# The lead-in of a hybrid GLA/Hyena layer rearranged: no identity products, a fourth ada buffer, filters and spectra later, eight shift pieces moved to the gate stage

## What is computed

```python
sh1, sc1, g1, sh2, sc2, g2 = modulation(c, w_ada, b_ada)     # silu(c) @ w_ada + b_ada, w_ada is 2048 x 12288
csh1, csc1, ... = modulation(c_ctx, w_ada, b_ada)
hc = rmsnorm(ctx, norm_pre_mix) * (1 + csc1) + csh1           # context: k, v and decay only
hx = rmsnorm(x, norm_pre_mix) * (1 + sc1) + sh1
x = x + g1 * rmsnorm(mixer(hx, states(hc)), norm_post_mix)    # mixer: h @ w_in (2048 x 10272), then
#   GLA branch, Hyena branch (filters from a sine network, long convolution through a DFT),
#   merge gates, p_gla, p_hy, w_out
hx = rmsnorm(x, norm_pre_ffn) * (1 + sc2) + sh2
x = x + g2 * rmsnorm((silu(hx @ ffn_gate) * (hx @ ffn_up)) @ ffn_down, norm_post_ffn)
```

## Time and profile before

| | us |
|---|---|
| median of three runs | 1625.83 (1625.36 to 1626.21) |
| the profiled execution | 1625.28 |
| its span, first to last instruction | 1623.5 |
| PE busy | 1587.5 (98%) |
| DVE busy | 1101.5 (68%) |
| ACT busy | 749.4 (46%) |
| mean granted clock of PE | 0.995 |

### The profile page before, as it was taken

How to read it: one execution, slowest core, us unless ns; L and a number is a source line. 1 busy time by engine, 2 the same in 40 slices (tenths; PEclk the granted TensorE clock), 3 DMA queues, 4 the chain that set the end, 5 groups by cost and what they waited for, 6 DMA issues and landing times.

```text
span 1623.5 us, 22521 instructions
## 1 busy us (share of the span) xinstructions
PE 1587.5 (98%) x8524; PEld 1302.6 (80%) x8524; DVE 1101.5 (68%) x1320; ACT 749.4 (46%) x901; POOL 81.0 (5%) x156
## 2 busy tenths in 40 slices
PE   6999999999999999999998999999999999999998
PEld 3556677888888888888887888888888888888886
DVE  3677777678789868778777666666666555555556
ACT  5442326643444434444446544555545544444444
POOL 0011120000000000100000000000000000000000
PEclk9999999999999999999999999999999999999999
DMA  9989958666577768966885777777776665565653
GB/s 332 327 299 379 326 191 280 187 202 202 178 244 222 229 200 267 297 225 217 292 298 178 233 237 231 244 230 235 237 234 198 186 191 197 193 193 192 194 193 121
DMA packets 264769, 377.74 MB, mean 233 GB/s; under 512 B 14161, under 2 KB 223420, under 8 KB 263164
## 3 DMA queue, kind: packets, MB, share of 16 engines
q1 hardware_dynamic: 243008, 297.57, 58.2%
q0 software_dynamic: 20800, 78.91, 14.3%
q10 hardware_dynamic: 892, 0.33, 0.1%
HBM read 372.57 MB, written 4.19 MB: 232 GB/s over the span
## 4 chain that ended last, share of the span: by engine, by line
PE 92%; DVE 3%; DMA 2%; ACT 1%; issue 1%; ACTq 0%; DVEq 0%
PE ps L1664 39%; PE ps L1671 19%; PE ps L1679 9%; PE ps L1681 8%; PE ps L1680 8%; PE ps L1604 2%; DMA a2k<-in_w_ada 1%; DVE acck L1048 1%; PE ps L1803 1%; PE ps L1815 0%; PE ps L1594 0%; PE ps L1841 0%; DVE lo L1116 0%; PE ps L1766 0%; PE ps L1833 0%
## 5 line engine op out<-in xcount | busy, mean ns | idle before, releaser
L1441 DVE TENSOR_TENSOR lo<-raw,hi 128x1024 fp32r<-128x1024 f32 x252 | 308.3, 1224 | 247.9 <-ACT hi L879 247.5
L1664 PE MATMUL ps<-hx,hi 128*128 128x512 f32 x1392 | 438.0, 396 | 1.5 <-DVE lo L1441 0.8
L879 ACT ACTIVATE hi<-raw 128x1024 fp32r<-128x1024 f32 x252 | 266.7, 1060 | 317.0 <-PE ps L1671 203.9
L625 ACT ACTIVATE hi<-raw 128x1024 fp32r<-128x1024 f32 x224 | 236.6, 1060 | 277.9 <-PE ps L1671 163.9
L1664 PE MATMUL ps<-hxc,hi 128*128 128x512 f32 x1088 | 346.0, 399 | 0.0
L1116 DVE TENSOR_TENSOR lo<-raw,hi 128x1024 fp32r<-128x1024 f32 x224 | 269.5, 1220 | 67.3 <-ACT hi L625 67.2
L1671 PEld LDWEIGHTS ps<-hx,lo 128*128 128x128 f32 x1408 | 264.5, 188 | 62.5
L1671 PE MATMUL ps<-hx,lo 128*128 128x256 f32 x1408 | 276.6, 278 | 0.0
L1671 PEld LDWEIGHTS ps<-hxc,lo 128*128 128x128 f32 x1088 | 204.4, 188 | 48.3
L1664 PEld LDWEIGHTS ps<-hx,hi 128*128 128x128 f32 x1392 | 212.0, 189 | 2.8 <-DVE lo L1441 1.0
L1671 PE MATMUL ps<-hxc,lo 128*128 128x256 f32 x1088 | 213.9, 278 | 0.0
(11 more groups left out here) (323 smaller groups left out, 1685.8 us busy)
## 6 DMA issues: line engine op xcount, KB each, us to landing
raw<-in_w_in SPq DMA_DIRECT2D x160, 512.0 KB, 4.6
a2raw<-in_w_ada POOLq DMA_DIRECT2D x96, 512.0 KB, 5.1
raw<-in_ffn_gate SPq DMA_DIRECT2D x88, 512.0 KB, 4.4
raw<-in_ffn_up SPq DMA_DIRECT2D x88, 512.0 KB, 4.4
raw<-in_ffn_down SPq DMA_DIRECT2D x88, 512.0 KB, 4.6
ada_raw<-in_w_ada SPq DMA_DIRECT2D x64, 512.0 KB, 10.1
a2k<-in_w_ada POOLq DMA_DIRECT2D x32, 512.0 KB, 6.7
raw<-in_w_out SPq DMA_DIRECT2D x32, 512.0 KB, 5.3
```

Of the source, the lines that this page charges most:

```text
L625: nc.scalar.activation(high_of(uu), raw[:, slot_of(uu), :], ACT.Copy).then_inc(hi_done, 1)
L879: nc.scalar.activation(hi[:, slot, :], raw[:, uu % RING, :], ACT.Copy).then_inc(hi_done, 1)
L1441: V.tensor_tensor(lo[:, uu % RING, :], raw[:, uu % RING, :], hi[:, uu % 4, :].bitcast(f32), SUB).then_inc(lo_done, 1)
L1664: mm(bank(b + t), (hi[:, uu % 4, :] if w_h is None else w_h)[:, c0:c0 + P], feat[:, k, :], start=first, stop=False)
```

## The change

It rearranges the lead-in and the kv stage:

- The 24 identity products (`keep_running`) go. Ada unit 0 comes ahead of the second turn, the turns of the first tokens come behind ada unit 2, and the third sine step moves behind the second kv piece.
- `ada_raw` gets a fourth buffer, used by ada unit 3 alone, in a part of the weight ring not yet in use; SP issues four ada units at once, and its order through block 1 is written out.
- Filter pairs 0 and 1 stand behind kv pieces 4 and 6 of block 1, pairs 2 and 3 in block 2; the eight spectra start at piece 5 of block 2. Filter tiles shrink to half. The stores of the spectra have a semaphore each.
- In block 0 to 2, ada units, turns and columns are placed anew; on DVE `columns(b+1)` comes ahead of the low part and the a2 piece at the same place.
- Only 24 of the 32 shift pieces stay in the kv stage, from block 2 on. The last eight become pieces 56 to 63 with a sum of their own (`acck2`), in the gate stage: `A2_AT` has 20 pieces on units 137 to 157, where it had 13 on units 138 to 158, 3 on 162 to 182 for 5, and 17 on 192 to 217 for 14 on 198 to 218. Eight more column sums and one DVE operation at the FFN's start bring them in.

```diff
-        A2_KV = [(), (7, 9, 11), (1, 3, 5, 7, 9, 11), (1, 3, 5, 7, 9, 11), (1, 9, 11),
-                 (1, 3, 5, 7, 9, 11), (1, 3, 5, 7, 9, 11), (1, 3)]
+        A2_KV = [(), (), (7, 9, 11), (1, 4, 6, 9, 11), (1, 4, 9, 11), (0, 1, 2, 4, 9, 11),
+                 (2, 6, 10), (1, 2, 4)]
         A2_AT = ([28 + int(2.4 * a) for a in range(19)] + [81, 86, 91, 96, 99, 102, 105, 108, 110, 112, 119, 121, 123]
-                 + [138 + int(1.7 * a) for a in range(13)] + [160 + 6 * a for a in range(5)]
-                 + [198 + int(1.6 * a) for a in range(14)])
+                 + [137 + int(1.1 * a) for a in range(20)] + [162, 172, 182]
+                 + [192 + int(1.6 * a) for a in range(17)])
...
-        AFTER = [{3: "a", 5: "xa", 7: "at", 8: "a", 9: "c"},
-                 {2: "a", 4: "a", 6: "a", 8: "a", 9: "tc"},
-                 {0: "a", 1: "at", 3: "a", 5: "a", 7: "c", 10: "a"}]
+        AFTER = [{5: "axa", 7: "at", 8: "a", 9: "c"},
+                 {1: "a", 3: "a", 5: "a", 7: "a", 8: "t", 9: "c"},
+                 {0: "a", 1: "a", 3: "a", 5: "a", 6: "t", 7: "c", 10: "a"}]
...
-        FILT_AFTER = [{}, {0: 0, 2: 1, 4: 2, 6: 3}] + [{}] * (NB - 2)
-        SPEC_AFTER = {0: 0, 1: 1, 2: 2, 3: 3, 4: 4, 6: 5, 8: 6, 11: 7}
+        FILT_AFTER = [{}, {4: 0, 6: 1}, {1: 2, 3: 3}] + [{}] * (NB - 3)
+        SPEC_AFTER = {(2, 5): 0, (2, 6): 1, (2, 7): 2, (2, 8): 3, (2, 9): 4, (2, 10): 5, (2, 11): 6,
+                      (3, 0): 7}
...
+        def ada_slot(n):
+            return n if n < 4 else (n - 4) % 3
...
             pool.wait_ge(t_sem["a"], upto(START, "a", startno("sine", 2)))
-            pool.wait_ge(kv_pe, 12)
+            pool.wait_ge(kv_pe, 20)
             pool.dma_start(cp[:, K_FWD:K_SEL], k_pack[:, K_FWD:K_SEL]).then_inc(s_fwd, 16)
+            pool.wait_ge(kv_pe, 26)
-            for a in range(7):
+            for a in range(4):
                 a2_load(a)
...
-                if b == 5:
+                if b == 6:
                     ins = shift_sums(16)
...
+                for j in range(8):
+                    ins = mm(bank(0)[:, KD + j:KD + j + 1], acck2[:, P * j:P * (j + 1)],
+                             ones[:, 0:1], start=True, stop=True)
...
             start_step("turn", 0)
+            pe.wait_ge(t_sem["a"], 1)
+            ada_unit(0)
             start_step("turn", 1)
             start_step("sine", 0)
-            pe.wait_ge(t_sem["a"], 1)
-            ada_unit(0)
-            keep_running(4)
             ada_unit(1)
-            keep_running(4)
             start_step("sine", 1)
+            ada_unit(2)
             turn_tokens(0, range(2))
             turn_tokens(1, range(2))
-            ada_unit(2)
-            keep_running(6)
             ada_unit(3)
-            keep_running(2)
-            start_step("sine", 2)
             columns(0)
-            keep_running(8)
```

More of the change, by code:

```diff
@@ L199, in layer @@
         s_win = sem("s_win")
-        ada_in = [sem(f"ada_in{i}") for i in range(3)]
+        ada_in = [sem(f"ada_in{i}") for i in range(4)]
         ada_mm, ada_rows = sem("ada_mm"), sem("ada_rows")
@@ L215, in layer @@
         a2_done = sem("a2_done")
-        s_wgz, s_kks, s_kkl, s_inv = sem("s_wgz"), sem("s_kks"), [sem(f"s_kkl{i}") for i in range(2)], sem("s_inv")
+        s_wgz, s_kks, s_kkl, s_inv = sem("s_wgz"), [sem(f"s_kks{i}") for i in range(2)], [sem(f"s_kkl{i}") for i in range(2)], sem("s_inv")
         s_row = [sem(f"s_row{i}") for i in range(4)]
@@ L426, in weight_load, with filter_load @@
                 sp.dma_start(dst, srcw).then_inc(arrival(uu)[0], 16)
-            for n in range(3):
+            def filter_load():
+                for half in range(2):
+                    sp.dma_start(outw[HID * half:HID * (half + 1), :],
+                                 out_w[:, HY * half:HY * (half + 1)]).then_inc(s_win, 16)
+                sp.dma_start(win[:], k_win.rearrange("(t p) n -> p t n", p=P)).then_inc(s_win, 16)
+            for n in range(4):
                 ada_load(n)
-            ada_load(3)
             weight_load(0)
@@ L435, in _ @@
             sp.dma_start(toks[:, 3, :], ctxt[P:2 * P, :]).then_inc(s_ctx[1], 16)
-            for b in range(NB - 1):
+            for n in range(4, 8):
+                ada_load(n)
+            weight_load(3)
+            ada_load(8)
+            ada_load(9)
+            weight_load(4)
+            filter_load()
+            ada_load(10)
+            weight_load(5)
+            ada_load(11)
+            weight_load(6)
+            weight_load(7)
+            sp.dma_start(lrw[:], w_in.rearrange("(k p) n -> p k n", p=P)
+                         [:, :, C_LR:C_LR + 2 * RANK]).then_inc(s_lrw, 16)
+            weight_load(8)
+            for b in range(2, NB - 1):
                 for n in range(3):
@@ L517, in _ @@
             pool.wait_ge(kv_ev, 12 * (NB - 1))
-            for a in range(32, 53):
+            for a in range(NKS, 45):
                 a2_load(a)
@@ L532, in _ @@
             pool.dma_start(grow[:], b_ada[:, 2 * D:3 * D].broadcast_to([P, D])).then_inc(s_row[0], 16)
-            for a in range(61, 64):
+            for a in range(53, 56):
                 a2_load(a)
@@ L536, in _ @@
             pool.dma_start(acc[:], n_post_mix.broadcast_to([P, D])).then_inc(s_row[1], 16)
-            for a in range(64, 84):
+            for a in range(56, 84):
                 a2_load(a)
@@ L679, in _ @@
             first_modulate(1, 0)
+            start_step("sine", 1)
             cut_high(1)
@@ L708, in _ @@
                 cut_high(3 * b + 3)
-                if b == 2:
-                    for m in range(5):
-                        spectrum(m)
+                if b == 3:
+                    spectrum(7)
                 cut_high(3 * b + 4)
@@ L1024, in filter_pair @@
-                V.tensor_tensor(filt_o[:, i, cols], filt_f[:, cols], filt_b[:, cols], SUB
-                                ).then_inc(flt_dve, 1)
+                    link(V.memset(filt_b[0:1, :], 0.0))
+                V.tensor_tensor(filt_e[:, i, cols], filt_f[:], filt_b[:], ADD)
+                V.tensor_tensor(filt_o[:, i, cols], filt_f[:], filt_b[:], SUB).then_inc(flt_dve, 1)
             def a2(a):
-                r = a % 32
+                chunk, half, k, src, dst = a2_part(a)
                 dve.wait_ge(a2_in[a % 2], 16 * (a // 2 + 1))
[L1031 to L1034, removed]
-                else:
[L1036 to L1043, removed]
@@ L1134, in _ @@
             unit_low(1)
+            normalize(0, slice(256, D))
             unit_low(2)
+            start_step("sine", 2)
             inverse(1)
             normalize(1, slice(0, 256))
-            normalize(0, slice(256, D))
             first_features(0, 1)
@@ L1150, in _ @@
                     kv_evac(b, idx)
-                    if b == 1 and idx == 0:
-                        unit_low(5)
+                    if b < NB - 1 and idx == MOD_AT[b]:
+                        columns(b + 1)
+                    if b == 1 and idx in (1, 5):
+                        unit_low(4 + idx // 5)
                     if idx in FILT_AFTER[b]:
@@ L1621, in columns @@
                     ins = turn(bank(6)[:, P * r:P * (r + 1)], modrow[:, P * r:P * (r + 1)], ident)
-                if b == 5:
+                if b == 6:
                     ins = shift_sums(16)
                 ins.then_inc(ada_cols, 1)
-            def keep_running(n):
-                for _ in range(n):
-                    mm(bank(1)[:, 0:P], ident, ident, start=True, stop=True)
             def turn_tokens(k, tiles=range(4)):
@@ L1893, in _ @@
                         filter_pair(FILT_AFTER[b][idx])
-                    if b == 2 and idx in SPEC_AFTER:
-                        spectrum(SPEC_AFTER[idx])
+                    if (b, idx) == (0, 1):
+                        start_step("sine", 2)
+                    if (b, idx) in SPEC_AFTER:
+                        spectrum(SPEC_AFTER[b, idx])
             for uu in range(NKV, NM - NW):
```

143 lines of the change are left out of this document (75 added, 68 removed).

## The result

The changed kernel takes 1643.6 us (median of five runs, 1638.48 to 1646.93), beside 1626.21 (1625.36 to 1627.87) for the kernel before: a ratio of 1.0105, 95% interval 1.009 to 1.012. It is 1% slower, 18.7 us above the forecast and above the range.

The account below looks back on a forecast made before the run. TensorE (PE), busy 98% of the span, bounds the kernel, with slack mostly before 90 us. Terms: -6.6 up to the main stage, +5.2 gate stage, +0.5 w stage, sum -0.9, so 1624.9 us; range 1617.5 to 1634.

Parts of the forecast that it names:

- Steps 1 to 3: Lead-in (-1.4 and +0.7 us), slow clock at kv's start (+2.4), filter and other waits around block 1 gone (-7.1, -0.3).
- step 2: Start of kv: PE at 1.2 GHz for 4 to 7 us, 46% of that lost, +2.4 us; by the skill never 0.
- Step 4: Rest of kv: fewer a2 pieces and feature waits, but a late sixteenth piece; -0.9 us, bounds -2.4 and +2.
- Step 5: Gate stage: eight pieces return, loads landing in L = 5.4 us hold DVE and PE's low parts; +5.2 us.
- Rival A: Gate stage is free, L near 4.7 or below or covered by PE's lead: 1619.7 us, chance 0.27.
- rival B: Gate stage is the new bound, loads landing in L = 6.8 us: 1637.5 us, slower, chance 0.15.
- Step 6: W stage and FFN's start: pieces from unit 192, load of x behind five more; +0.5 us (0 to 3), FFN start 0.
- Rival C: Clock costs more: gate-stage stalls drop it, or kv's slow start meets a second one; 1630.5 us, chance 0.12.
- step 3: Second kv block: filter pairs split over blocks 1 and 2, so filter and feature waits and slow clock go; -7.1 and -0.3 us.

Follow-up runs that it names:

- the kernel with the w stage emptied: Changed kernel with the w stage as before the change (14 pieces from unit 198), six pieces at 162 to 187 for three: 1636.81 us, ratio 1.0063.
- the kernel placed anew: Changed kernel with a2 pieces spread in kv blocks 5 and 7, gate pieces at 1.7 units, w stage as before the change: 1617.68 us, ratio 0.9964.
- both kv bursts spread: Changed kernel with the a2 pieces of kv blocks 5 and 7 spread, the rest kept: 1628.8 us over ten runs, ratio 1.002.
- 1.4 units: The changed kernel with all a2 placings mended, but its 20 gate-stage pieces 1.4 units apart for 1.7: 1617.04 us, ratio 0.9956.

## Why the prediction was wrong

**Steps 1 to 3 came out, as a sum.** They make -5.7 us; measured are -8.4 at block 2, with two filter pairs still to come, and -5.9 at block 5. kv started at 30.41 for 30.0, at half clock for 6.8 us, inside the 4 to 7 us of step 2. Its "never 0" did not hold in every execution: the kernel with the w stage emptied, whose lead-in is the changed kernel's, was granted 1.00 from 24 us to 181 in its profiled execution, and so was the kernel placed anew. The filter waits are gone. That the filters' new places are what gave the 7.1 us rests on the ladder and on the waits that vanished, not on an experiment.

**Step 4 failed: "the sixteenth then ends some 1.5 us after PE wants its sums in columns(6). -0.9 us; bounds -2.4 and +2."** It cost 12.8 us. Three things were wrong. The wait was 3.10 us for 1.5. Of the difference 0.7 is the load of the sixteenth piece, 7.5 us for the 6.8 taken; the prediction doesn't show its count, so the rest stays open. And it was costed as a wait alone: PE at half clock for 9.2 us behind it lost another 4.2 (46%, by step 2's own ratio). Then block 7's (1, 2, 4) was not worked out at all, though the last shift sums wait for it: 4.29 us, and 6.8 us at half clock, 3.1 more. That makes 3.1 + 4.2 + 4.3 + 3.1 = 14.7, less the 2.4 of the feature waits, which did go: 12.3 of 12.8. The experiments bear it out: with both bursts spread, units 32 to 136 stand 16 us earlier.

**Step 5 was right in its mechanism and its waits.** L was 5.3 (5.4 taken), the waits for `lo` 5.0 us in four places ("some five times, 5 us in all"). The stage cost 7.7 for the 5.2 forecast: 1.6 more came from 3.4 us at half clock, and 1.1 is left over. Rival A fails here on its L, and rival B, whose 1637.5 lies nearest to the result, has the wrong cause: L is not near 6.8.

**Step 6 was too small: +0.5 (0 to 3) for 5.0.** The load of `x` did delay the next, as it said, but by some 8 us: 14.3 us to landing where 6.2 is the median of the kernel before. PE waited 3.2 us and lost 1.6 more to the clock. At the FFN's start PE waited 1.4 us for 3.6 before, but was at half clock for 10.2 us for 6.8; that stretch cost 2.1 where 0 was forecast. The other runs separate it: from unit 223 to the end of the span a profiled execution lost 0.5 us on the kernel before where that slow stretch was 6.8 us long (both kv bursts spread, and 1.4 units), 2.1 at 10.2 us (the kernel placed anew), and 3.7 at 13.7 us (w stage emptied). So 1.6 of the 2.1 is the clock.

**Rival C was the right kind** ("PE's stalls of 1 to 2 us in the gate stage drop it, as at 64.95, once or twice at 3 us") at too low a price, and for the gate stage and the start of kv alone: there were 17 us of half clock in the rest of kv, 3.4 in the gate stage, 3.4 in the w stage. The prediction had both facts, from the earlier trace rows: a wait of 2.4 us, then some 7 us slow. It used them at the start of kv and in step 3, and not for the waits that it forecast itself in steps 4 and 5. The Trainium skill, "TensorE: Matmul & The Clock Gate", section "Part 1: The HAM clock gate", has it that an idle PE goes back to the slow clock; the trace agrees at 184.24 and 233.78, behind waits of 3.10 and 4.29 us.

## What to carry to other kernels

- Cost a stall of a full-speed PE as its length and, as an estimate from the waits here, some three quarters again. Here waits of 3.10, 4.29, 1.81 and 3.17 us, 12.4 in all, came with 10.2, 6.8, 3.4 and 3.4 us at half clock, 23.8 in all, of which 46% is 10.9. A wait of 1.88 us came with none. So 14.3 us of waits cost 10.9 more, but singly between nothing and one and a half times their length: a risk to price and not a certainty.
- A chain on two buffers keeps up when its places are (landing + issue + operation)/2 apart; they can be closer only by what the consumer's lead covers over the whole row. Keep sums that PE waits for away from the end of a burst of such pieces, and small loads that are needed soon from behind a large one in the same queue.
- A change whose work is right can lose by a table of places: the same change, with only two tables laid anew, went from 1.0105 to 0.9964 of the time before.

## What the runs showed of the hardware

- In the changed kernel a wait of 1.81 us (at 694.65) was followed by 3.4 us at half clock, one of 3.10 us by 10.2 us, and one of 1.88 us (at 651.68) by none. With the w stage emptied, a wait of 2.01 us (at 646.82) had none behind it either.
- The same wait does not always leave the clock low. The kernel placed anew waits 2.6 us for `hxc` ahead of kv like the changed one, but was granted 1.00 in 28 to 38 in its profiled run, where the changed kernel had 0.66. The executions of the changed kernel spread with the clock: 1638.5 us at a mean granted clock of 0.991, and 1646.9 at 0.986. What decides it stays open.
- Behind a load of 2 MB in POOL's queue, which took 13.6 us, two loads of 512 KB took 14.3 and 10.5 us; the two after them took 5.0 and 4.4.
